# Two feed-forward up projections move from one level of seven products to two levels

## What is computed

```python
def swiglu(h, w_in, w_out):
    gt, up = jnp.split(h @ w_in, 2, axis=-1)
    return (jax.nn.silu(gt) * up) @ w_out
```

## Time and profile before

| | us |
|---|---|
| three runs: median (lowest to highest) | 3931.96 (3931.93 to 3935.13) |
| profiled execution, first to last instruction | 3933.3 |
| stage `up0`, from its first product to the first of `down0` | 398.8 |
| stage `up1`, the same | 268.9 |

### The profile page before, as it was taken

One profiled execution on the slowest core, in us unless ns is written; L12 is line 12 of the kernel. 1 busy time (PEld: TensorE's weight loads), 2 busy tenths in 40 slices (PEclk: granted clock), 3 DMA queues, 4 the chain that ended last, 5 costly groups with the idle time before them and its releaser, 6 DMA issues.

```text
span 3933.3 us, 48502 instructions
## 1 busy us (share of the span) xinstructions
PE 3827.1 (97%) x18602; PEld 2867.3 (73%) x18602; DVE 2221.4 (56%) x3856; ACT 741.8 (19%) x1402; POOL 716.2 (18%) x570
## 2 busy tenths in 40 slices
PE   7999988999999999999999999999999999999998
PEld 3455567665555555688888877888789998778886
DVE  4255677354445313326564755654888888556546
ACT  2144455211110013421100000000311111100002
POOL 0048844000000000000000002120244343121200
PEclk9999999999999999999999999999999999999999
DMA  5244400222121121122322322232222222122321
GB/s 193 88 169 150 139 2 2 86 84 56 55 62 59 48 75 43 33 65 79 91 74 89 95 77 86 85 102 86 77 73 72 69 69 64 54 86 85 102 86 65
DMA packets 381407, 312.13 MB, mean 79 GB/s; under 512 B 9552, under 2 KB 349904, under 8 KB 381136
## 3 DMA queue, kind: packets, MB, share of 16 engines
q1 hardware_dynamic: 381264, 310.16, 25.3%
HBM read 308.03 MB, written 2.10 MB: 79 GB/s over the span
## 4 chain that ended last, share of the span: by engine, by line
PE 87%; POOL 5%; DVE 3%; ACT 2%; issue 1%; DMA 1%; POOLq 0%; SPq 0%; DVEq 0%; ACTq 0%
PE ps_lin L967 18%; PE ps_lin L867 10%; PE ps_d L967 9%; PE ps_lin L1741 6%; PE ps_d L867 5%; PE ps_c L967 4%; PE ps_lin L750 4%; PE ps_lin L767 3%; PE ps_d L750 3%; PE ps_lin L813 3%; PE ps_lin L1158 3%; PE ps_c L867 3%; POOL arena L3507 2%; PE ps_d L1530 2%; POOL arena L3504 2%; PE ps_c L750 2%
## 5 line engine op out<-in xcount | busy, mean ns | idle before, releaser
L3476 POOL TENSOR_TENSOR rstd<-square 128x512 f32<-128x512 f32 (+2 forms) x12 | 15.1, 1260 | 1542.5 <-ACT square L1919 1542.5
L967 PE MATMUL ps_lin<-arena,ring 128*128 128x256 f32 (+1 forms) x800 | 217.2, 424 | 1.1 <-DVE arena L2598 1.1
L867 PE MATMUL ps_lin<-arena,ring 128*128 128x256 f32 (+1 forms) x864 | 214.1, 401 | 0.0
L967 PEld LDWEIGHTS ps_lin<-arena,ring 128*128 128x128 f32 x800 | 151.8, 190 | 60.9 <-issue 2.9
L867 PEld LDWEIGHTS ps_lin<-arena,ring 128*128 128x128 f32 x864 | 164.2, 190 | 41.1
L967 PE MATMUL ps_lin<-hid_in,arena 128*128 128x256 f32 x832 | 188.6, 380 | 3.6 <-DVE arena L2625 3.6
L3479 POOL TENSOR_TENSOR rstd<-rstd,square 128x512 f32<-128x512 f32 (+2 forms) x58 | 75.5, 1301 | 630.9 <-ACT square L1919 630.0
L967 PE MATMUL ps_lin<-hid_in,mixed 128*128 128x384 f32 (+1 forms) x672 | 187.7, 432 | 0.0
L967 PE MATMUL ps_d<-arena,mixed 128*128 128x384 f32 (+1 forms) x672 | 187.7, 432 | 0.0
L2622 DVE TENSOR_TENSOR arena<-ring 128x1024 f32<-128x1024 f32 x84 | 102.9, 1225 | 146.3 <-PE ps_d L867 135.9
L967 PEld LDWEIGHTS ps_lin<-hid_in,arena 128*128 128x128 f32 x832 | 157.7, 190 | 27.7 <-DVE arena L2625 5.6
(11 more groups left out here) (546 smaller groups left out, 8101.4 us busy)
## 6 DMA issues: line engine op xcount, KB each, us to landing
ring<-in_ffn_w_in SPq DMA_DIRECT2D x88, 512.0 KB, 4.8
resid<-in_ada_w SPq DMA_DIRECT2D x20, 2048.0 KB, 7.9
ring<-in_mlp_w_up SPq DMA_DIRECT2D x64, 512.0 KB, 4.5
ring<-in_mlp_w_down SPq DMA_DIRECT2D x64, 512.0 KB, 4.4
ring<-in_attn_w_qkv SPq DMA_DIRECT2D x64, 512.0 KB, 4.8
ring<-in_ffn_w_out SPq DMA_DIRECT2D x32, 512.0 KB, 4.4
ring<-in_even_w_in SPq DMA_DIRECT2D x28, 512.0 KB, 5.0
ring<-in_sc_w_in SPq DMA_DIRECT2D x24, 512.0 KB, 4.6
```

Of the source, the lines that this page charges most:

```text
L867: last = mm(prod[i - 1], lhs[:, j, :], rhs(p), start=(g == j == 0), stop=(g == G - 1 and j == np_ - 1))
L967: last = mm(out, lhs[:, j, :], rhs[:, j, :], start=(j == 0), stop=(j == 3))
```

## The change

The up projections work in 11 *rounds* of 256 gate and 256 up columns (what two slots did). The outer level is the seven-product form with fewer additions (four sums of weights S1 to S4, four of inputs T1 to T4, seven additions of results), on blocks of 256 weight columns, 512 features and half the tokens. An outer product is either made *whole*, as two tiles of four matmuls of half the tokens, or *split*: into seven inner products of two matmuls of a quarter of the tokens (192 columns in `up0`, 128 in `up1`). In round 0 nothing is split. In rounds 1 to 10 six of seven are split, in both stages; product 4 is whole. Outer products are numbered by n through the stage, 77 of them; in rounds 1 to 10 a round has the positions p = 0 to 6 for products 1, 2, 6, 7, 4, 5, 3.

Inner products 1, 6, 7 and 4 accumulate one after the other in one PSUM bank, and ScalarE copies the bank between them; 5 and 3 share another bank. VectorE makes four half sums of weights for each split product, three blocks of its result (`11`, `22`, `12`; ScalarE copies the fourth), and the outer additions. All of it is unrolled; the loops are gone. The rest of the diff joins pairs of semaphores under one name with the counts added up (`const_rest` and `wg_in` to `rest_in`, `v0_in` and `v1_in` to `v_in`, `angle` and `trig` to `turned`, `mod_in` to `raw_in`). Sums that the old scheme made of the inputs are dropped; in round 0 and at n = 7 and 8 VectorE makes quarter sums of the inputs instead (`inner_inputs`, four operations for each of six blocks).

```diff
-STAGES = [("even_qk", 3), ("up0", 22), ("down0", (4, 4, 3)), ("up1", 22), ...
+STAGES = [("even_qk", 3), ("down0", (4, 4, 3)), ("down1", (4, 4, 3)), ...
+TWO_WIDTH, ROUNDS = {"up0": T, "up1": LAT}, KF // 2
+OUTERS = 7 * ROUNDS
+ORDERS = ((1, 2, 3, 6, 7, 4, 5), (1, 2, 6, 7, 4, 5, 3))
+ADDITIONS = ({2: [(2, 1)], 6: [(6, 1)], 7: [(7, 6), (3, 6)], 4: [(4, 7)], 5: [(7, 5), (3, 5)]},
+             {2: [(2, 1)], 6: [(6, 1)], 7: [(7, 6)], 4: [(4, 7)], 5: [(7, 5), (6, 5)], 3: [(3, 6)]})
+IN_SEVEN = {"up0": (1, 2, 6, 7, 5, 3), "up1": (1, 2, 6, 7, 5, 3)}
+SPLIT_AT = {1: 1, 2: 2, 4: 6, 5: 7, 7: 5, 8: 3}
```

SyncE, `up_phase` (the loads of a round):

```diff
+                for r in (1, 2):
+                    half_done(prev)(r - 1)
+                    for c in (1, 2):
+                        fill(0, r, c)
+                for i in range(1, ROUNDS):
+                    sp.wait_ge(s.two_added, ADDED[st, i - 1, "S3"])
+                    sp.wait_ge(s.two_made, used(st, index_of(i - 1, 1)))
+                    fill(i, 1, 1)
+                    sp.wait_ge(s.two_added, ADDED[st, i - 1, "S4"])
+                    sp.wait_ge(s.two_made, used(st, index_of(i - 1, 2)))
+                    fill(i, 1, 2)
+                    sp.wait_ge(s.two_made, used(st, index_of(i - 1, 7)))
+                    fill(i, 2, 1)
+                    sp.wait_ge(s.two_made, used(st, index_of(i - 1, 4)))
+                    fill(i, 2, 2)
```

TensorE, `two_level`; `seventh(n, j)` is inner product j of outer product n, two matmuls:

```diff
+                    if j == 5:
+                        pe.wait_ge(s.two_added, ADDED[st, n, "half", 1])
...
+                    if j == 6:
+                        pe.wait_ge(s.two_taken, TAKEN[st, n, 1])
+                        pe.wait_ge(s.two_added, ADDED[st, n, "half", 2])
+                    if j == 7:
+                        pe.wait_ge(s.two_taken, TAKEN[st, n, 2])
+                        pe.wait_ge(s.two_added, ADDED[st, n, "half", 3])
+                    if j == 4:
+                        pe.wait_ge(s.two_taken, TAKEN[st, n, 3])
+                    if j == 3:
+                        pe.wait_ge(s.two_added, ADDED[st, n, 22])
+                        pe.wait_ge(s.two_added, ADDED[st, n, "half", 4])
...
+                for n in range(OUTERS):
+                    if split(st, n):
+                        seventh(n, 1)
+                        seventh(n, 2)
+                    else:
+                        whole(n, "a")
+                    if n == 0:
+                        square_sum(late, None)
+                    if split(st, n - 1):
+                        seventh(n - 1, 4)
+                    if split(st, n):
+                        seventh(n, 6)
+                        seventh(n, 5)
+                    else:
+                        whole(n, "b")
+                    if split(st, n - 1):
+                        seventh(n - 1, 3)
+                    if split(st, n):
+                        seventh(n, 7)
+                seventh(OUTERS - 1, 4)
+                seventh(OUTERS - 1, 3)
+                pe.wait_ge(s.two_taken, TAKEN[st, OUTERS - 1, 4])
+                pe.wait_ge(s.two_added, ADDED[st, OUTERS - 1, 12])
```

ScalarE, `two_level`; `partial(n, k)` copies the bank after inner products 1, 6 and 7, `last_block` after 4, `gates` are two Silu:

```diff
+                for n in range(OUTERS):
+                    if split(st, n):
+                        partial(st, n, 1)
...
+                    if split(st, n - 1):
+                        last_block(st, n - 1)
+                    if split(st, n):
+                        partial(st, n, 2)
+                        partial(st, n, 3)
...
+                    if n % 7 == 0 and n:
+                        gates(st, n // 7 - 1)
```

VectorE, the end of `split_norm`, in place of the old sums of inputs and weights (`input_blocks` makes T1, T2, T3, S3 and T4, in this order):

```diff
+                weights_sum(stage, 0, "S1")
+                weights_sum(stage, 0, "S2")
                 scaled(late, range(KD))
+                weights_sum(stage, 0, "S4")
+                input_blocks(stage, late)
```

VectorE, `halves`, four sums of 128x256 from a product's weights:

```diff
+                    if k == 1:
+                        last = tt(w[1], a21, a22, add)
+                    elif k == 3:
+                        last = tt(w[3], a11, a21, sub)
+                    elif k == 2:
+                        dve.wait_ge(s.two_added, ADDED[st, n, "half", 1])
+                        last = tt(w[2], w[1], a11, sub)
+                    else:
+                        dve.wait_ge(s.two_added, ADDED[st, n, "half", 2])
+                        last = tt(w[4], a12, w[2], sub)
```

VectorE, `block_of`; `22` is the bank of inner product 5 plus the third copy, `12` the same bank after inner product 3 plus the second copy, `11` inner product 2 plus the first copy:

```diff
+                elif which == 22:
+                    dve.wait_ge(s.two_made, MADE[st, n, 5])
+                    dve.wait_ge(s.two_taken, TAKEN[st, n, 3])
+                    last = tt(out[:, 1, q:2 * q], fifth, part[2], add)
+                else:
+                    dve.wait_ge(s.two_made, MADE[st, n, 3])
+                    dve.wait_ge(s.two_taken, TAKEN[st, n, 2])
+                    last = tt(out[:, 0, q:2 * q], fifth, part[1], add)
```

VectorE, `two_level`:

```diff
+                for n in range(OUTERS):
+                    i, p = divmod(n, 7)
+                    if split(st, n - 1):
+                        block_of(st, n - 1, 22)
+                    if split(st, n):
+                        block_of(st, n, 11)
+                    if i and p < 3:
+                        weights_sum(st, i, ("S1", "S2", "S3")[p])
+                    if split(st, n + 1):
+                        halves(st, n + 1, (1, 3, 2))
+                    if split(st, n - 1):
+                        block_of(st, n - 1, 12)
+                    if split(st, n + 1):
+                        halves(st, n + 1, (4,))
+                    if i and p == 4:
+                        weights_sum(st, i, "S4")
+                    if n:
+                        outer_adds(st, n - 1)
+                    if i and 0 < p < 3:
+                        gated_tile(st, i - 1, p - 1)
...
+                block_of(st, OUTERS - 1, 22)
+                dve.wait_ge(s.two_made, MADE[st, index_of(ROUNDS - 1, 4), "b"])
+                down_sums(following, 0)
+                block_of(st, OUTERS - 1, 12)
+                outer_adds(st, OUTERS - 1)
+                for t in range(2):
+                    gated_tile(st, ROUNDS - 1, t)
```

More of the change, by code:

```diff
@@ new lines, with outer, index_of, additions @@
+IN_SEVEN = {"up0": (1, 2, 6, 7, 5, 3), "up1": (1, 2, 6, 7, 5, 3)}
+INNER_SUMS = (1, 3, 2, 4)
+BLOCK_OF = {1: "B11", 2: "B21", 3: "B22", 4: "T4", 5: "T1", 6: "T2", 7: "T3"}
+SUM_OF = {6: "S2", 7: "S3", 5: "S1", 3: "S4"}
+SPLIT_AT = {1: 1, 2: 2, 4: 6, 5: 7, 7: 5, 8: 3}
+def outer(n):
+    return ORDERS[int(n >= 7)][n % 7]
+def index_of(i, x):
+    return 7 * i + ORDERS[int(i > 0)].index(x)
+def additions(n):
+    return ADDITIONS[int(n >= 7)].get(outer(n), [])
+def split(st, n):
+    return 7 <= n < OUTERS and outer(n) in IN_SEVEN[st]
@@ L1512, in _ @@
             split_phase("even_out", 1)
-            strassen("up0", T, "ffn0", over=False)
+            two_level("up0", "ffn0")
             down_phase("down0")
@@ L1654, in _ @@
             split_phase("odd_out", 2)
-            strassen("up1", LAT, "ffn1", over=False)
+            two_level("up1", "ffn1")
             down_phase("down1")
@@ L2565, in split_norm @@
                     added(late, k)
-                for j, (b11, b12, b21, b22) in enumerate(blocks):
-                    dve.wait_ge(s.h_new, H_COUNT[first] - KD + 2 * j + 2)
-                    tt(b21_11[:, j, :], b21, b11, sub).then_inc(s.u_bs, 1)
-                for k in (5, 6):
+                for k in range(5, KD):
                     added(late, k)
-                dve.wait_ge(ring_full[0], 32 * (FILLS[stage] + 1))
-                tt(ws["sum"], r1, r2, add).then_inc(s.made_early, 1)
@@ new lines, in outer_adds @@
+            def outer_adds(st, n):
+                i = n // 7
+                of = {outer(7 * i + k): destination(st, 7 * i + k) for k in range(7)}
+                if additions(n) and split(st, n):
+                    dve.wait_ge(s.two_taken, TAKEN[st, n, 4])
+                    dve.wait_ge(s.two_added, ADDED[st, n, 12])
+                elif additions(n):
+                    dve.wait_ge(s.two_taken, TAKEN[st, n, "b"])
+                for to, x in additions(n):
+                    if (to, x) in ((7, 6), (6, 5)):
+                        dve.wait_ge(s.two_added, added_at(st, i, 6, 1))
+                    if (to, x) == (3, 6):
+                        dve.wait_ge(s.two_added, added_at(st, i, *((6, 5) if i else (6, 1))))
+                    if (to, x) == (4, 7):
+                        dve.wait_ge(s.two_added, added_at(st, i, 7, 6))
+                    if (to, x) == (7, 5):
+                        dve.wait_ge(s.two_added, added_at(st, i, 4, 7))
+                    if (to, x) == (3, 5):
+                        dve.wait_ge(s.two_added, added_at(st, i, 3, 6))
+                    tt(of[to], of[to], of[x], add).then_inc(s.two_added, 1)
@@ L2707, in gated, with combine @@
                 return f
-            def combine(stage, u, outs, width, first=False):
+            def combine(stage, u, outs, width):
                 _, base, ev, _ = STRASSEN[stage]
@@ L2738, in slot @@
                 def slot(i, sl):
-                    first = stage in ("up0", "up1") and isinstance(i, int) and i == sl == 0
```

(2 more changed lines are left out.)

464 lines of the change are left out of this document (350 added, 114 removed).

## The result

The changed kernel takes 3946.2 us (median of 7 runs, 3942.1 to 3948.4) where the kernel before takes 3932.9 (7 runs beside it): 1.003 times as long, 95% interval 1.0021 to 1.0039. It is slower by 13 us, 0.3%. The forecast was 3927, no change that can be told; the range, up to 3950, held the time, the sign was wrong.

What follows compares the result with a forecast made beforehand. TensorE, busy for 97% of the span, was taken as the bound. -29 + 0.8 + 2 + 3.5 = -23 us for `up0` and +13 - 1.6 + 3 + 4 = +18 for `up1` gave -5: 3927 us, range 3899 to 3950.

Steps and rivals of the forecast that it cites:

- Weights: Weight loads in each round: third load lands some 6 us after S4, VectorE has 6.2 us of work in `up1`; no stall.
- TensorE's side: Matmul time in both stages: 0.327 us at 192 columns, 0.223 at 128; a round 32.6 us in `up0`, 22.2 in `up1`.
- VectorE's side: VectorE's work in a round: 25.5 us in `up0` (before 16.0), 21.8 in `up1` (before 13.3).
- third rival: VectorE's operations in both stages don't overlap, each pays its whole duration; +47 us in all, 3979 us; chance 0.10.
- interlock: TensorE and VectorE waiting for each other: rounds of 33.2 us in `up0` (-29 over ten), 25.5 in `up1` (+13).
- leg through product 4: `up1`, from block `22` of position 2 to block `12` of position 3: VectorE waits on TensorE's work, 5.87 us a round.
- first rival: VectorE keeps up in `up1`: a round takes 22.8 us, -14 in place of +13; 3900 us; chance 0.27.
- second rival: Late weights: S1 waits 2 us for its third load in every round of `up1`, +20; 3947 us; chance 0.15.
- Start: Beginning of each stage, with round 1's quarter sums: +0.8 and +2 us in `up0`, -1.6 and +3 in `up1`.
- End: End of each stage, where input sums for the down stage delay the last block `12`: +3.5 us in `up0`, +4 in `up1`.

Runs made afterwards that it cites:

- e2: Changed kernel with the two loads that S1 needs issued ahead of the load that waits for S4; 3936.0 us, 1.0006 to the kernel before.
- e1: Changed kernel with S4 made ahead of block `12` of position 3 instead of behind it; 3927.3 us, 0.9984 to the kernel before.
- e5: e1 with inner product 3 of position 3 made between the two halves of whole product 4; 3928.5 us, 0.9986 to the kernel before.
- e9: e1 with S1, S2 and S3 made for 16 of 256 columns in later rounds of `up1`, so part is not computed; 3909.6 us.
- e6: Changed kernel with half sums, weight sums and outer additions narrowed in later rounds of `up1`, so part is not computed; 3908.4 us.
- e11: Changed kernel with nine matmuls that nothing reads at the end of both `up0` and `up1`; 3941.0 us, 1.0017 to the kernel before.
- e3: Changed kernel with no product of `up1` split, `up0` as it was; 3913.5 us, 0.995 to the kernel before.
- e4: Changed kernel with four products split in `up1`, those at positions 0 and 1 left whole; 3926.4 us, 0.9983 to the kernel before.
- e8: e4 with S4 made early as in e1; 3922.9 us, 0.9974 to the kernel before.
- e10: e3 with nine matmuls that nothing reads at the end of `up0`; 3912.2 us, 0.9943 to the kernel before.

## Why the prediction was wrong

The forecast's span was 3928 and the trace has 3944.3, 16 us more; what was forecast as no change came out slower. Two steps failed: Weights, where no stall was taken, and the end of the stages, where no term stood for the clock. The steps in their order:

- **TensorE's side** was right. Groups of four records of 192 columns start 0.65 us apart, 0.325 a matmul (forecast 0.327); 128 columns give 0.223.

```profile
1083.83 0.81 PE L1251 MATMUL ps_d<-hid_in,ring 128*128 128x192 f32 x4
1084.48 0.81 PE L1251 MATMUL ps_lin<-const,arena 128*128 128x192 f32 x4
1085.13 0.81 PE L1251 MATMUL ps_lin<-arena 128*128 128x192 f32 x4
```

- **VectorE's side** was right within 3%: it worked for 250.7 us of `up1`, where the forecast's 85% of 287 are 244, and half sums that need nothing from one another start 0.33 us apart. The third rival, 0.41 between them, is out. It went by the first half of what the Trainium skill says in "VectorE: DVE Perf Modes", section "The DRAIN you can't avoid", that the next operation does not start until the pipe is empty; the trace agrees with the second half, that an operation which nothing holds starts earlier.
- **The interlock** was right: `up0` 33.0 us a round (33.2), with TensorE idle only ahead of inner product 6 of position 1 until its last product; `up1` 25.6 (25.5) once the loads are out of the way (e2). The leg through product 4, from block `22` of position 2 at 1845.50 to block `12` of position 3 at 1851.38, is 5.88 us long, forecast 5.87. What the forecast did not see is that another bound stood 0.7 us below it, the lag of positions 0 to 2 by itself (e1, e5, e9). The first rival, VectorE keeping up, is what e6 and e9 show with work left out, 23.1 us; the whole work does not get there.
- **Weights** is the step that failed. It took 6 us from S4 to the third load, against 6.2 us of VectorE's work, and no stall. VectorE's work was as said, 6.5 us in the round shown; the third load landed 7.1 to 8.2 us behind S4's end in the nine rounds. The step's own terms, 0.46 for an issue, 4.4 for a landing and 1.4 for a third load, make 6.3, which already left no margin. The 1.4 was right: the third load landed 1.3 to 1.4 us behind the second. The 4.4 was mis-sized: it came from loads issued in pairs, and with three the second landed 5.8 to 6.9 us behind S4 and not 4.9. The wait costs 1.07 us a round and 10.2 us in all by e2. The second rival named this mechanism and its place at twice the price (2 us a round, 3947); its chance of 0.15 was too low for such a margin. That 3946 was measured is luck for it: the loads gave half of its 20 us, less than the 1.3 us a round from which it decides, and the clock brought much of the rest.
- **Start** and **End** were right in `up0` (376.1 us, forecast 375.8), though in part by luck: its later rounds are 0.2 us shorter each than forecast and round 1 is 1.3 us longer, which nearly cancel. What stood in no step is the clock behind the end: the forecast had TensorE's idle time there but took the next stage at full clock. It is 2.1 us more between the stages and 3.1 more behind `up1`, of which e11 gave back about 5.

Loads +10.2, clock about +5, small rests in `up1` +2, and `up0` with its earlier start -1.5: that is the 16 us; the rests were not traced further. Neither of the first two alone would have taken the forecast's -5 past the +7.9 that can be told from no change. With the loads put right the kernel is where the forecast had it, no change that can be told (e2, 1.0006); with the clock alone put right it is still slower, by 0.17% (e11).

The split itself was worth what the forecast said in each stage: -23 us in `up0`, a loss in `up1`. Hence e3: split where VectorE has room.

## What to carry to other kernels

Where a sum of small terms leaves a margin of 0.2 us between a load and its user, in every round, the load is not hidden; look at the queue's order first, since a load whose wait comes late holds all that stand behind it, and putting the ones that are needed first ahead cost nothing here and gave 10 us. When a finer scheme trades one engine's time for another's, compare the two engines stage by stage: the same edit gave 23 us where VectorE's 25.5 us of a round stood beside TensorE's 32.6, and lost 30, a third of it to the loads, where 21.8 stood beside 22.2 with in-order waits both ways. Idle time at a stage's end can cost more than its length, since the next stage may start at half the clock.

## What was not expected of the hardware

TensorE's granted clock after one and the same idle time was not always the same. In ten traces with the 2.33 us of idle at the end of `up0` unfilled (the changed kernel, e1 to e9), `down0` kept full clock in three (e1, e4, e5) and fell to half for 2.8 to 6.1 us in the other seven; after the 2.47 us (e6: 2.42) at the end of a split `up1`, `down1` kept full clock in two (e1, e8) and fell to half for 3 to 5.5 us in the other seven. It fell in none of the places where TensorE's wait there was 1.49 us (e3) or filled down to 0.33 to 0.46 (three places in e10 and e11), nor in the kernel before, where it had none. So a single profile of such an end can differ by some 3 us from the next for this alone.

Loads of 512 KB that are issued close together also land later, the first one too. With the next issue 1.7 us behind it, it landed after 3.4 to 3.6 us in eight of nine rounds (e2); with one more 0.4 us behind it, after 3.9 to 4.4 (e1); with two more, after 4.3 to 5.5 (the changed kernel). These cases differ in what else moved at the time, and no run took that apart.
